# One decoder layer on one core: VectorE's order in the attention phase, bias behind maxima, normalisation two slots behind, a tile's close one slot later

## What is computed

```
def masked_softmax(s, mask):
    s = jnp.where(mask, s.astype(jnp.float32), -jnp.inf)
    m = jnp.max(s, axis=-1, keepdims=True)
    m = jnp.where(jnp.isfinite(m), m, 0.0)
    e = jnp.exp(s - m)
    return e / jnp.maximum(jnp.sum(e, axis=-1, keepdims=True), 1e-30)
...
    p_c = masked_softmax(s, cmp_end[None, :] <= t[:, None])
    o_c = jnp.einsum('bgrqn,bgnd->bgrqd', p_c.astype(dt), cv)
...
    s = jnp.einsum('bgrqd,bgqkd->bgrqk', qi, ksel) * scale
    p_s = masked_softmax(s, smask[:, :, None])
    o_s = jnp.einsum('bgrqk,bgqkd->bgrqd', p_s.astype(dt), vsel)
...
    s = jnp.einsum('bgrqd,bgkd->bgrqk', qi, kwi) * scale
    p_w = masked_softmax(s, wmask)
    o_w = jnp.einsum('bgrqk,bgkd->bgrqd', p_w.astype(dt), vwi)
...
    o = (gates[..., 0:1] * unblock(o_c) + gates[..., 1:2] * unblock(o_s)
         + gates[..., 2:3] * unblock(o_w))
```

## Time and profile before

| what | value |
|---|---|
| time, median of 3 runs | 1783.72 us (1783.25 to 1783.78) |
| span of the profiled execution, first to last instruction | 1782.5 us |
| around the span (median less span) | 1.2 us |
| TensorE busy over the span | 1653.7 us (93%) |
| VectorE busy over the span | 1054.2 us (59%) |
| ScalarE busy over the span | 628.0 us (35%) |
| attention (450 to 770 us): TensorE, VectorE, ScalarE busy | 294.6, 285.5, 230.5 us of 320 |
| mean granted TensorE clock | 0.975 of full speed |

### The profile page before, as it was taken

The page is one execution under the profiler, slowest core; times in us unless marked ns, Lnnn a source line. Parts: engine busy times, 40 slices in busy tenths (PEclk is TensorE's granted clock), DMA queues, the critical chain, the costliest instruction groups (busy, mean ns, idle before and its releaser), DMA issues.

```text
span 1782.5 us, 22209 instructions
## 1 busy us (share of the span) xinstructions
PE 1653.7 (93%) x8157; PEld 1334.8 (75%) x8157; DVE 1054.2 (59%) x2073; ACT 628.0 (35%) x1161; POOL 109.5 (6%) x132
## 2 busy tenths in 40 slices
PE   3999999998789999989899999999999999996894
PEld 1888888888656776668788888888888888885673
DVE  7542556565799999842545556556555555556233
ACT  5103443344577777731422212212212212213121
POOL 4101112121000000000100000000000000000002
PEclk9999999999699999999899999999999999998997
DMA  5233323225000000130211211211111112102002
GB/s 188 90 100 120 102 93 110 78 80 200 24 22 16 13 13 1 65 138 0 75 55 36 71 35 38 68 35 46 60 35 52 54 35 57 61 1 95 0 36 82
DMA packets 47850, 110.57 MB, mean 62 GB/s; under 512 B 8864, under 2 KB 17056, under 8 KB 47776
## 3 DMA queue, kind: packets, MB, share of 16 engines
q1 hardware_dynamic: 40352, 85.47, 14.8%
q0 software_dynamic: 7424, 24.12, 4.0%
HBM read 89.65 MB, written 19.92 MB: 61 GB/s over the span
## 4 chain that ended last, share of the span: by engine, by line
PE 81%; DVE 11%; ACT 3%; DMA 2%; issue 2%; POOL 0%; POOLq 0%; SPq 0%; DVEq 0%; ACTq 0%
PE ps L1325 27%; PE ps L1011 13%; PE ps L1012 13%; PE ps L1013 13%; PE ps L1146 3%; PE ps L1262 3%; PE ps L1219 2%; PE ps L1225 1%; PE ps L1264 1%; PE ps L1016 1%; DVE xtl L1444 1%; PE ps L1169 1%; DVE wl L1424 1%; DVE htl L1612 1%; PE ps L1265 1%
## 5 line engine op out<-in xcount | busy, mean ns | idle before, releaser
L1798 DVE TENSOR_TENSOR h<-h,ps 128x512 f32<-128x512 f32 x352 | 236.1, 685 | 156.1 <-PE ps L1013 154.8
L1325 PE MATMUL ps<-hth,wuh 128*128 128x512 f32 x704 | 218.6, 392 | 3.1 <-DVE wul L1612 3.1
L1325 PE MATMUL ps<-htl,wuh 128*128 128x512 f32 x704 | 219.0, 392 | 0.0
L1325 PE MATMUL ps<-hth,wul 128*128 128x512 f32 x704 | 218.6, 392 | 0.0
L1011 PE MATMUL ps<-wh,xth 128*128 128x512 f32 (+1 forms) x448 | 187.5, 419 | 31.1 <-DVE wl L1424 29.7
L1013 PE MATMUL ps<-wh,xtl 128*128 128x512 f32 (+1 forms) x448 | 171.2, 382 | 0.0
L1012 PE MATMUL ps<-wl,xth 128*128 128x512 f32 (+1 forms) x448 | 170.7, 381 | 0.0
L952 ACT ACTIVATE ffh<-ffa 128x1024 fp32r<-128x1024 f32 x22 | 23.3, 1059 | 385.1 <-DVE ffa L1815 385.1
L1325 PEld LDWEIGHTS ps<-hth,wuh 128*128 128x128 f32 x704 | 132.4, 188 | 32.9 <-issue 3.3
L1325 PEld LDWEIGHTS ps<-hth,wul 128*128 128x128 f32 x704 | 132.7, 188 | 29.4
L1325 PEld LDWEIGHTS ps<-htl,wuh 128*128 128x128 f32 x704 | 132.5, 188 | 28.8
(11 more groups left out here) (263 smaller groups left out, 3174.8 us busy)
## 6 DMA issues: line engine op xcount, KB each, us to landing
wuraw<-in_w_up SPq DMA_DIRECT2D x44, 512.0 KB, 5.4
wraw<-in_w_in SPq DMA_DIRECT2D x48, 256.0 KB, 3.2
proj_d<-stage POOLq DMA_DIRECT2D x48, 256.0 KB, 2.3
wdraw<-in_w_down SPq DMA_DIRECT2D x22, 512.0 KB, 3.5
rin<-proj_d POOLq DMA_DIRECT2D x32, 256.0 KB, 4.0
xraw<-in_xt SPq DMA_DIRECT2D x8, 512.0 KB, 4.9
h<-in_x SPq DMA_DIRECT2D x1, 4096.0 KB, 12.8
owraw<-in_w_out SPq DMA_DIRECT2D x16, 256.0 KB, 3.1
```

The source lines that it names most:

```text
L1325: mm = nc.tensor.matmul(ps[:, 2 * part + half, :], w_, x_[:, k, half * 512:(half + 1) * 512], start=(k == 0 and i == 0), stop=(k == NK - 1 ...
L1798: nc.vector.tensor_tensor(hh, hh, ps[:, 4 + o_ % 4, :], ALU.add).then_inc(dn_add, 1)
```

## The change

Four things are rewritten, all in the order; no instruction is added, removed or resized.

- VectorE's bias of step n stands directly behind the maxima of step n, ahead of the guard.
- Guard, inverse and normalisation are those of step n-2 instead of n-1.
- A slot's first low stands between the guard and the inverse, and a second one between the inverse and the normalisation. Before, all lows stood behind the inverse.
- The items that close a tile start one slot later, on every engine: `base` is 8(v+1)+2, and there is one slot more at the end. The splitting and turning of the next tile's queries stay in their slots.

```
-            slots = [[] for _ in range(per * (NV + 1) + 3)]
+            slots = [[] for _ in range(per * (NV + 1) + 4)]
...
-                base = per * (v + 1) + 1
+                base = per * (v + 1) + 2
...
                     maxima = row_max(*divmod(n, 2 * RG))
-                if 0 < n <= 2 * RG * NV:
-                    guarded = guard_sum(*divmod(n - 1, 2 * RG))
-                if n < 2 * RG * NV:
                     exp_bias(*divmod(n, 2 * RG), maxima)
-                if 0 < n <= 2 * RG * NV:
-                    inverted = invert_sum(*divmod(n - 1, 2 * RG), guarded)
-                for st in lows:
+                if 2 <= n < 2 * RG * NV + 2:
+                    guarded = guard_sum(*divmod(n - 2, 2 * RG))
+                for st in lows[:1]:
                     {"turn_p": p_low, "turn_ret": ret_low}[st[0]](st)
-                if 0 < n <= 2 * RG * NV:
-                    normalize(*divmod(n - 1, 2 * RG), inverted)
+                if 2 <= n < 2 * RG * NV + 2:
+                    inverted = invert_sum(*divmod(n - 2, 2 * RG), guarded)
+                for st in lows[1:]:
+                    {"turn_p": p_low, "turn_ret": ret_low}[st[0]](st)
+                if 2 <= n < 2 * RG * NV + 2:
+                    normalize(*divmod(n - 2, 2 * RG), inverted)
```

## The result

The changed kernel takes 1799.34 us (median of 4 runs, 1798.41 to 1800.78), the kernel before in the same comparison 1783.75 us. The ratio is 1.0082, 95% interval 1.0067 to 1.0098: **0.8% slower, some 15 us**. The span of the profiled execution grew from 1782.5 to 1797.8 us, by 15.3.

What follows compares the result with a forecast made beforehand. It took VectorE to bound the attention from 500 to 600 us, TensorE to 750, chains of waits before 500. Terms 7.5 + 3.7 + 1.5 - 0.7 + 0.5 = +12.5 us gave 1796 us, range 1783 to 1808.

Steps and rivals of the forecast that it cites:

- The bias ahead of the guard gains nothing: VectorE's slots: bias already starts 0.03 to 0.04 us behind its maxima; held guards worth at most 2 us.
- The count on VectorE: Bias to normalisation grows 0.19, 0.20 or 0.07 us with no, one or two lows; 23.5 us in all.
- idle time up by about 20 us: VectorE after the change: added idle time, in gaps too small to be listed as waits.
- What of it reaches the end: VectorE's cost reaching the end: +1.5 us from 450 to 500 us, +7.5 to 600, +3.7 to 750.
- two thirds of the growth: Attention some 12 us longer, two thirds of it before what was 600 us in the earlier trace.
- The close one slot later: Tile close moved on all engines: -0.7 us at the seams, +0.5 us at the beginning and end.
- -0.7 at the seams: Query rest leaves the path from last normalisation to `retl`; 3 x 0.42 us less longer maxima saved.
- +0.5 for the beginning and the end: One more slot without items at the beginning, one without scores at the end; bounds 0 and +1.5 us.
- a turned tile is as far behind its normalisation as it was: Tile close: the same items move on all engines, so that distance was claimed unchanged; no size given.
- The clock rival: TensorE's granted clock also falls from 500 to 560 us, two more dips: +24 us, 1807 us; chance 0.15.
- The rival of no cost: Dependences on VectorE cost nothing or TensorE hides them; only seams and ends remain: 1784 us; chance 0.13.
- The bound: Attention: VectorE sets the pace from 500 to 600 us, TensorE leads from 600 to 750, waits before 500.

Runs made afterwards that it cites:

- filled: Changed kernel with guard and inverse of step n-1, inverse behind the normalisation of n-2, so dependences are covered: 1783.19 us, ratio 1.0007.
- gaps_alone: Kernel before with only the new order inside a slot, still normalising step n-1, tiles closing where they did: 1796.75 us, ratio 1.0079.
- lag_alone: Kernel before, old order inside a slot, with guard, inverse and normalisation of step n-2 and tiles closing one slot later: 1785.44 us, ratio 1.0005.
- gaps_and_shift: Changed kernel with guard, inverse and normalisation of step n-1 in place of n-2: 1801.08 us, ratio 1.0098.
- shift_alone: Kernel before with only the close of the tiles one slot later, still normalising step n-1: 1787.27 us, ratio 1.0021.
- no_guard_even: Kernel before without the guard of even steps, the reciprocal taking its place: 1782.53 us, ratio 1.0000.
- staggered: Kernel before, old order inside a slot, normalising step n-2 with the inverse made a slot earlier, tiles closing one slot later: 1781.88 us, ratio 0.9995.
- stag_even: Kernel before with normalisation of n-2, inverse a slot earlier, later close, and no guard of even steps: 1779.45 us, ratio 0.9982.
- bias_first: Kernel before with only the bias moved ahead of the guard, lows left behind the inverse: 1797.14 us, ratio 1.0079.
- split_alone: Kernel before with only the lows moved, the first ahead of the inverse, the second behind it: 1788.60 us, ratio 1.0030.
- lag_no_guard_even: Kernel before with old order, guard, inverse and normalisation of n-2, later close, and no guard of even steps: 1782.63 us, ratio 0.9997.

## Why the prediction came out as it did

The time forecast was 1796, the measured one 1799.3: right in direction, in the main mechanism and, within 3.3 us, in size. That the smaller terms came so near in sum is partly luck, as shown below.

- **The bias ahead of the guard gains nothing: right.** It starts 0.03 us behind its maxima in both kernels, and with it moved alone the kernel loses 14.1 us.
- **The count on VectorE: right for each kind of slot, somewhat high in sum.** 0.48 for 0.47, 0.94 for 0.94 and 1.39 for 1.40 us in the three kinds of slot. Where it would show was half wrong: I said idle time up by about 20 us. VectorE's busy time grew by 10.8 us, because small instructions no longer overlap, and the idle time ahead of the four groups concerned (bias, inverse, both normalisations) by only some 8.5. Together that is 19 of the 23.5 us; where the rest went is open. One of the four groups in the changed kernel, against 0.0 us in the earlier trace rows:

```profile
L1668 DVE TENSOR_SCALAR nb<-mx 128x1 f32<-128x1 f32 (+1 forms) x128 | 20.7, 162 | 4.4
```

These 4.4 us are no loss by themselves: the bias stands as far behind its maxima as before, only the guard's tail no longer covers the 0.03 us between them. The line is the same in filled, which loses next to nothing.

- **What of it reaches the end: right in sum, with one wrong sign.** The three terms were 7.5 + 3.7 + 1.5 = 12.7 us; the new order costs 13.7 to 14.1 in three settings. gaps_alone, which has nothing else in it, gives +7.0, +5.1 and -1.3 us by stretch for +7.5, +3.7 and +1.5. The first stretch was thus mis-sized: what the bare dependences add there does not show, at a clock that also differs (0.76 against 0.68). I had said that two thirds of the growth would lie before what is step 76; in the changed kernel it is 6.6 of 13.5 us.
- **The close one slot later: both terms wrong, their sum nearly right by luck.** I took -0.7 at the seams and +0.5 for the beginning and the end. The -0.7 did not come: the late waits for `retl` are 5.1 us for 4.5. Instead TensorE's waits for normalisations rose from 1.6 to 11.4 us. The step that failed is "a turned tile is as far behind its normalisation as it was". In slots that is true; but the slot ahead of the seam is now an odd one. That parity is the cause was only argued: lag_alone has the same parity and 5.4 us of such waits, so that at most half of them come from it alone, and gaps_and_shift, which has hardly any of them, is no faster. The +0.5 was off at both ends. The end costs 3.8 us, of which 2.0 to 2.3 are in every other run with the later close. The beginning I had counted as a small loss, and it is a gain: the first stretch falls to 44.0 us in shift_alone and 44.5 in lag_alone, of which the clock may be a part. Net, close and lag cost 0.9 us with the old order and 14.6 - 14.1 = 0.5 with the new one, where I had -0.2.
- **The clock rival: seen, but not the cause.** There are dips behind four seams, and the mean clock of the changed kernel is 0.969 to 0.972 in its four runs, before 0.975 in the trace. But gaps_alone loses 14.1 us at an unchanged mean clock, and 7.0 of them in a stretch at full clock.
- **The rival of no cost**, with the rule of the Trainium skill that a semaphore between two VectorE instructions costs nothing (VectorE: DVE Perf Modes, "The DRAIN you can't avoid"), does not hold here: filled and the changed kernel have the same instructions, and covering the dependences is worth 13 us. For small instructions that follow what they need at once, the measurement decides.
- **The bound.** I wrote that VectorE sets the pace from 500 to 600 us. If it alone did, 8 to 12 us less on it would show; 0 to 3 came against the kernel before. All of these runs but no_guard_even have the later close and the lag in them, so the fair partner is lag_alone: against it 1.4 us came for 8, 1.8 for 7.5 (staggered) and 4.1 for 12 (stag_even), and only the last is clear of the noise. A saving thus counts for none to a third, where an addition counts for six to eight tenths (14.1 of 24 us in bias_first, 5.4 of 7 in split_alone). From step 29 to 76 the four runs that put less on VectorE (staggered, no_guard_even, stag_even, lag_no_guard_even) take 99.8 to 100.8 us, against 100.2 before and 101.3 in lag_alone. VectorE and the loop of TensorE and ScalarE being nearly equally long there would explain this; the waits that grow in lag_no_guard_even fit it, but no run shows it by itself.

Open remain 1.7 of the 3.7 us of the later close, which is about as much as its interval is wide to one side, and how much of the end's 3.8 us is the dip at 768 us. gaps_and_shift, with the same order and close, takes 26.0 us there where the changed kernel takes 27.6, so that lag and dip together come to some 1.6 us.

## What to carry to other kernels

Before reordering a busy engine's small instructions, write down for each what it needs and how far behind that it stands: here 0.07 us between independent ones and 0.20 between dependent ones, over 128 steps, was 14 of the 15 us. An instruction in the shadow of a long one, like the guard here, is free, and moving it out to let its neighbour start "earlier" gains nothing if that neighbour waits for the long one anyway. Where two engines are about equally busy, price additions and savings apart: here six to eight tenths of each us added reached the end, of 8 us taken away next to nothing, and of 12 us a third. And compare a run with the one that differs from it in a single thing: against the kernel before, the later close hid part of what the savings gave.

## What the hardware showed that I had not expected

A small VectorE instruction lasts 0.15 to 0.17 us in the profile, but a neighbour that doesn't need it starts 0.07 to 0.08 us behind it; about half its length is overlap that the busy time counts once. The overlap lost turned up as busy time, 1054.2 to 1065.0 us with the same 2073 instructions. A rise in an engine's busy time can therefore be a stall.
